# Hybrid attention and convolution layer: x loaded by channels, queries from rows not yet normalised, the operand rescaled later

## The chip, the cores and the metric

The kernel runs on one core of a Trainium2 chip. The metric is the device time of one execution in microseconds (us). Before the change three runs gave 733.79, 735.06 and 737.27 us, median 735.06.

## The reference

One decoder layer over 1024 tokens of 1024 channels. The rows are normalised, projected once, and the projection's columns go to two groups of heads: sparse attention (queries, three pairs of keys and values, gates) and a short gated convolution.

```python
h = rms_norm(x, norm_w)                       # x * rsqrt(mean(x*x) + eps) * norm_w
proj = einsum('bsd,de->bse', h, w_in)
q, kv_all, gate_logits, nsa_z, cv_h, cv_b, cv_c, cv_z = split(proj)
q = apply_rope(rms_norm(q per head, q_norm_w), pos)
k_c, v_c, k_s, v_s, k_w, v_w = split(kv_all, 6)
k_c = rope(rms_norm(compress_blocks(k_c, ...)));  v_c = compress_blocks(v_c, ...)
k_s, k_w = rope(rms_norm(k_s)), rope(rms_norm(k_w))
# compressed, selected and sliding-window attention, gated and summed
o_nsa = (g0 * o_cmp + g1 * o_slc + g2 * o_win) * silu(nsa_z)
o_conv = cv_b * (conv3(cv_c * cv_h) + conv_b) * silu(cv_z)
return x + concat(o_nsa, o_conv) @ w_out
```

Since the queries are normalised once more per head, the row's factor enters them only through the small eps; it is kept all the same, in the statistics.

## The kernel before

Every product is made of three matmuls over a high and a low part of each operand (`three`, L1221 to L1226): high by high, low by high, high by low. `hh` and `hl` are the two parts of the normalised x, stored by channels (128 channels by 1024 tokens, eight blocks), and `wh`, `wl` those of the weights, in two slots.

The first stage, up to about 195 us, works through a list of entries, `ENTRIES`, in this order: q (heads 0 to 3), kc (keys and values that are to be compressed), q (heads 4 to 7), w1 (first hidden layer), kv (selection keys and values), w1 (second hidden layer), kv (window keys and values, and gates), z. An entry of kind q or kv has eight items, one for each 128 tokens, of 256 or 280 columns; kc and z have four items of 512 columns. Items take turns in the four PSUM banks `pj`; an item may start when ScalarE (`act_rel`) and VectorE (`dve_rel`) have read the item that had its bank.

The opening: for each of eight token tiles a transfer brings 128 rows of x, ScalarE squares them with a running sum, VectorE makes the reciprocal standard deviation (`inv_std`) and scales the rows (L973), TensorE transposes them in eight matmuls (`x_transposes`, L1235), ScalarE casts the transposed tile to `hh` (L720) and VectorE subtracts to get `hl` (L980). One tile behind, TensorE computes the first q item.

The weights come in pieces through a ring of four raw buffers (`weights`): SyncE starts a transfer, ScalarE casts it to the high part (L633), GpSimd subtracts to get the low part (L535), and only then the buffer is loaded again. Each engine's order is written out by hand. VectorE normalises queries and keys in place when an entry is through (`normalise`: L916 to L920, L1000, L1001, L925 to L930), TensorE transposes the keys (`key_transposes`, L1294), ScalarE and VectorE split them (`key_hi`, `key_lo`). The kc items are copied into blocks (L666, L667, L955, L956), get a position added (L1042), are cast and subtracted (`block_hi` L695, `block_lo` L547) and feed the hidden layers.

Behind the first stage a main loop of steps does attention, side tiles (convolution and gates; `channels`, written to `pf`) and the output projection. The first side tile's matmuls and the first queries' transposes (L1306) open it.

Of the kernel before, what the change touches and what calls it, by code (L numbers as in the profile page):

```python
# [15 lines left out]
P = 128  # L16
# [17 lines left out]
ENTRIES = [("q", 0, 256, 0), ("kc", 512, 256, 0), ("q", 256, 256, 1), ("w1", 0, 256, 0),  # L34
           ("kv", 768, 256, 0), ("w1", 1, 256, 1), ("kv", 1024, 280, 1), ("z", 1304, 256, 0)]
# [6 lines left out]
PIECES = [5 if w == 280 else 4 for _, _, w, _ in ENTRIES]  # L42
# [7 lines left out]


# [199 lines left out]
def hybrid_layer(nc: bass.Bass, x, wpack, wside, wout, normw, qnorm, knorm, par, const, maskc, out):  # L251
    with ExitStack() as ctx:
# [11 lines left out]
        prm = sb("prm", [P, NPAR])  # L264
        kst = sb("kst", [P, 2, GROUPS, SEQ], F32R)
# [13 lines left out]
        with ExitStack() as c:  # L279
# [3 lines left out]
            with ExitStack() as d:  # L283
                wh, wl = [None, None], [None, None]
                for s in range(2):
                    wh[s] = sb(f"wh{s}", [P, NK * (280 - 24 * s)], F32R, d)
                    wl[s] = sb(f"wl{s}", [P, NK * (280 - 24 * s)], F32R, d)
                sq = sb("sq", [P, 512], F32, d)
# [3 lines left out]
                stat = sb("stat", [P, 5, 41], F32, d)  # L292
# [38 lines left out]
        x_in = [sem(f"x_in{s}") for s in range(2)]  # L331
# [3 lines left out]
        x_sq, x_std, x_norm = sem("x_sq"), sem("x_std"), sem("x_norm")  # L335
        xt_done, hh_ready, hl_ready = sem("xt_done"), sem("hh_ready"), sem("hl_ready")
# [41 lines left out]
        xtile = lambda t: stage[:, (t % 2) * SEQ:(t % 2 + 1) * SEQ]  # L378
        krow = stage.rearrange("p (t g u d) -> p t g u d", t=NT, g=GROUPS, u=2)
        blocks = [mixn[:, 2 * f:2 * f + 2, :] for f in range(2)]  # L380
        hid = mixn[:, 0, 0:4 * P].rearrange("p (a c) -> p a c", a=4)
        ckr = mixn[:, 1, 0:2 * HD].rearrange("p (u d) -> p u d", u=2)
        cksq = mixn[:, 1, 2 * HD:3 * HD]
        cktmp = mixn[:, 1, 256:288].rearrange("p (a r) -> p a r", a=4)
# [11 lines left out]
        def entry_through(eng, e):  # L396

            if ENTRIES[e][0] == "w1":
                eng.wait_ge(hid_done, ENTRIES[e][3] + 1)
            else:  # L400
                eng.wait_ge(item_done, first_item[e + 1])
# [36 lines left out]
        def half_free(eng, h):  # L438

            if h < 3:  # L440
                entry_through(eng, NE - 2)
# [9 lines left out]
        def _(sp):  # L451
            sp.dma_start(xtile(0), x[0:P, :]).then_inc(x_in[0], 16)
            sp.dma_start(cst[:, :], const).then_inc(const_in, 16)
            sp.dma_start(mixc[:, 0, :], normw.to_broadcast([P, DM])).then_inc(normw_in, 16)
            sp.dma_start(xtile(1), x[P:2 * P, :]).then_inc(x_in[1], 16)
# [10 lines left out]
            for p in range(4):  # L466
                weights(p)
            sp.dma_start(prm[:, :], par).then_inc(param_in, 16)
            sp.dma_start(hnorm[:, 0, :], qnorm.to_broadcast([P, HD])).then_inc(param_in, 16)
            for b in range(3):  # L470
                sp.dma_start(hnorm[:, 1 + b, :], knorm[b:b + 1, :].to_broadcast([P, HD])).then_inc(param_in, 16)
            sp.dma_start(maskb[:, :].bitcast(U16), maskc).then_inc(masks_in, 16)
            for t in range(2, NT):
                sp.wait_ge(xt_done, 2 * (t - 2) + 2)
                sp.dma_start(xtile(t), x[t * P:(t + 1) * P, :]).then_inc(x_in[t % 2], 16)
                if t == 4:
                    for p in range(4, 8):
                        weights(p)
            for p in range(8, FIRST_PIECE[NE]):
                weights(p)  # L480

            entry_through(sp, NE - 2)
# [38 lines left out]
        def _(pool):  # L521
# [9 lines left out]
            def weights(p):  # L531
                e, j = PIECE_OF[p]
                w = piece_width(e)
                pool.wait_ge(wh_ready, p + 1)
                nc.gpsimd.tensor_tensor(wl[e % 2][:, j * w:(j + 1) * w], raw[p % 4][:, 0:w],  # L535
                                        wh[e % 2][:, j * w:(j + 1) * w].bitcast(F32), ALU.subtract)\
                    .then_inc(wl_ready, 1)

# [33 lines left out]
            for e in range(NE):  # L572
                for p in range(FIRST_PIECE[e], FIRST_PIECE[e + 1]):
                    weights(p)
                if e == 2:
                    block_lo(0)
                if e == 4:
                    block_lo(1)
            for h in range(3):
                half_lo(h)  # L580
            entry_through(pool, NE - 1)
# [39 lines left out]
        def _(act):  # L621
            A = nc.scalar.activation

            def weights(p):
# [4 lines left out]
                w = piece_width(e)  # L629
                act.wait_ge(raw_in[p % 4], 16 * (p // 4 + 1))  # L630
                if e >= 2:
                    entry_through(act, e - 2)
                nc.scalar.copy(wh[e % 2][:, j * w:(j + 1) * w], raw[p % 4][:, 0:w]).then_inc(wh_ready, 1)  # L633

            def pieces(e):

                return range(FIRST_PIECE[e], FIRST_PIECE[e + 1]) if e < NE else ()

            def item(e, m):
# [3 lines left out]
                bank = pj[n % 4]  # L643
                act.wait_ge(item_done, n + 1)
                if kind in ("q", "kv"):
                    tk = n - sum(items_of(a) for a in range(e) if ENTRIES[a][0] not in ("q", "kv"))
                    w = 256 if kind == "q" else 128
                    if tk >= 2:
                        act.wait_ge(sq_read, tk - 1)
                    A(sq[:, (tk % 2) * 256:(tk % 2) * 256 + w], bank[:, 0:w], ACT.Square).then_inc(sq_ready, 1)  # L650
# [890 lines left out]
```

## Time and profile before

| what | value |
|---|---|
| median of three runs | 735.06 us |
| the profiled execution | 732.45 us, span 730.7 us |
| TensorE busy | 681.3 us, 93% of the span |
| VectorE busy | 468.9 us, 64% |
| ScalarE busy | 372.7 us, 51% |
| GpSimd busy | 197.7 us, 27% |
| mean granted TensorE clock | 0.995 of 2.4 GHz |
| end of the first stage (first side tile) | 194.75 us |

How to read it: the page tells each engine's busy time over the whole span. Matmuls are pipelined, so the distance between their starts, not the duration shown, is what each one costs. In the rows below PE is TensorE, DVE VectorE, ACT ScalarE, POOL GpSimd; L is a line of the kernel; names are those of the program (`qp` holds raw weights, queries and keys, `xt` and `pj` are PSUM banks). A time in brackets is the engine's idle time ahead of the instruction, with what ended it.

### The profile page before, as it was taken

To read this page: it belongs to the slowest core of one execution; us is meant where nothing else is said; L and a number is where in the kernel's file an instruction comes from. 1 tells how busy PE (TensorE), PEld (TensorE's weight loads), DVE (VectorE), ACT (ScalarE), POOL (GpSimd) and SP (SyncE) were. 2 spreads that over 40 slices of the span, in tenths; PEclk is the share of its full clock that TensorE was granted. 3 is DMA by queue.
4 is the path that set the end of the run, shared out by engine and by line. 5 is a ranking of instruction groups with operands and counts; after the bars stand their busy time and mean duration, and the time that the engine had idled before them with its cause. 6 is when DMAs were issued, how large, how long until landed. Compare 5 with 4: busy or idle time off the path is not lost.

```text
span 730.7 us, 10838 instructions
## 1 busy us (share of the span) xinstructions
PE 681.3 (93%) x3791; PEld 575.9 (79%) x3791; DVE 468.9 (64%) x1147; ACT 372.7 (51%) x905; POOL 197.7 (27%) x220
## 2 busy tenths in 40 slices
PE   2899999889999999999998999889899999999997
PEld 1888899888788788878876788778677888888775
DVE  4777454645234655577667787687878777777752
ACT  5652535442334434436564565645677555555541
POOL 2112454520223223133121232211376021212120
PEclk9999999999999999999999999999999999999999
DMA  6521131400111111111100111000042011110101
GB/s 223 174 87 30 30 101 27 110 1 30 44 30 46 42 30 44 31 44 29 30 16 14 30 31 30 14 30 31 33 140 88 30 44 44 44 44 30 59 29 58
DMA packets 19206, 36.85 MB, mean 50 GB/s; under 512 B 2640, under 2 KB 3536, under 8 KB 19152
## 3 DMA queue, kind: packets, MB, share of 16 engines
q1 hardware_dynamic: 19152, 36.15, 15.8%
q8 instruction: 31, 0.51, 0.3%
q14 instruction: 23, 0.19, 0.1%
HBM read 31.95 MB, written 4.19 MB: 49 GB/s over the span
## 4 chain that ended last, share of the span: by engine, by line
PE 75%; DVE 13%; issue 5%; ACT 5%; DMA 2%; POOL 1%; SPq 0%; ACTq 0%; DVEq 0%; POOLq 0%
PE pf L1224 9%; PE pf L1225 9%; PE pf L1226 9%; PE tp L1455 7%; PE po L1435 5%; PE pj L1224 5%; PE pj L1225 5%; PE pj L1226 5%; PE sc L1315 4%; PE po L1436 4%; PE sc L1314 4%; PE sc L1224 3%; PE sc L1226 3%; PE sc L1225 3%; DVE sc L1144 1%
## 5 line engine op out<-in xcount | busy, mean ns | idle before, releaser
L837 ACT CAST pth<-tp 128x512 fp32r<-128x512 f32 (+1 forms) x148 | 86.7, 586 | 130.9 <-PE tp L1455 130.4
L1144 DVE CUSTOM_DVE_ANT_0 sc<-sc,maskb 128x64 f32<-128x64 f32 (+8 forms) x192 | 102.8, 563 | 57.0 <-PE sc L1315 56.6
L1163 DVE TENSOR_TENSOR ptl<-tp,pth 128x512 fp32r<-128x512 f32 (+1 forms) x148 | 102.0, 689 | 45.7 <-ACT pth L837 44.8
L594 POOL TENSOR_SCALAR qp<-qp,precip,gate 128x64 f32<-128x64 f32 x64 | 38.2, 598 | 207.4 <-DVE precip L1134 207.2
L1455 PE MATMUL tp<-cst,qp 128*128 128x128 f32 (+1 forms) x592 | 88.8, 272 | 3.6 <-issue 2.7
L552 POOL TENSOR_TENSOR fl<-fraw,fh 128x512 fp32r<-128x512 f32 x36 | 47.6, 1323 | 127.9 <-ACT fh L702 127.9
L1224 PE MATMUL pf<-hh,fh 128*128 128x512 f32 x200 | 81.2, 406 | 0.8 <-DVE ub L1103 0.8
L1224 PE MATMUL pj<-wh,hh 128*128 128x256 f32 (+1 forms) x256 | 75.5, 295 | 6.7 <-POOL wl L535 5.4
L1455 PEld LDWEIGHTS tp<-cst,qp 128*128 128x128 f32 (+1 forms) x592 | 68.9, 137 | 13.3 <-issue 3.4
L1225 PE MATMUL pf<-hl,fh 128*128 128x512 f32 x200 | 78.8, 394 | 0.0
L1226 PE MATMUL pf<-hh,fl 128*128 128x512 f32 x200 | 78.6, 393 | 0.0
L1225 PE MATMUL pj<-wl,hh 128*128 128x256 f32 (+1 forms) x256 | 73.9, 289 | 0.0
L1226 PE MATMUL pj<-wh,hl 128*128 128x256 f32 (+1 forms) x256 | 73.7, 288 | 0.0
L1435 PE MATMUL po<-pth,val 128*128 128x512 f32 x132 | 62.9, 477 | 7.6 <-DVE ptl L1163 4.5
L535 POOL TENSOR_TENSOR wl<-qp,wh 128x512 fp32r<-128x512 f32 (+1 forms) x33 | 45.7, 1410 | 89.1 <-ACT wh L633 89.1
L1140 DVE TENSOR_SCALAR qp<-qp,precip,gate 128x640 f32<-128x640 f32 (+7 forms) x96 | 57.8, 602 | 3.6
L1224 PEld LDWEIGHTS pj<-wh,hh 128*128 128x128 f32 x256 | 49.9, 195 | 9.0 <-issue 7.6
L1314 PE MATMUL sc<-kst,qh 128*128 128x512 f32 (+3 forms) x152 | 51.8, 341 | 2.8 <-DVE ql L1016 2.2
L1315 PE MATMUL sc<-kst,ql 128*128 128x512 f32 (+3 forms) x152 | 52.1, 345 | 0.0
L1436 PE MATMUL po<-ptl,val 128*128 128x512 f32 x132 | 52.1, 395 | 0.0
L1224 PE MATMUL pf<-woh,msh 128*128 128x512 f32 x120 | 49.1, 409 | 2.8 <-POOL wol L606 2.6
L1225 PEld LDWEIGHTS pj<-wl,hh 128*128 128x128 f32 x256 | 49.9, 195 | 0.0
(185 smaller groups left out, 1556.3 us busy)
## 6 DMA issues: line engine op xcount, KB each, us to landing
fraw<-in_wside SPq DMA_DIRECT2D x36, 256.0 KB, 2.7
qp<-in_wpack SPq DMA_DIRECT2D x28, 256.0 KB, 3.1
qp<-in_x SPq DMA_DIRECT2D x8, 512.0 KB, 3.3
wor<-in_wout SPq DMA_DIRECT2D x16, 256.0 KB, 2.8
xo<-in_x SPq DMA_DIRECT2D x16, 256.0 KB, 2.8
out<-xo SPq DMA_DIRECT2D x16, 256.0 KB, 2.0
qp<-in_wpack SPq DMA_DIRECT2D x5, 224.0 KB, 2.6
maskb<-in_maskc SPq DMA_DIRECT2D x1, 544.0 KB, 5.8
```

The costliest lines, as they stand in the source:

```text
L837: nc.scalar.copy(pth[ptn % 2][0:r, :], tp[tpn % 2][0:r, :]).then_inc(pth_ready, 1)
L1140: V.tensor_scalar(p, p, factor, main, ALU.mult, ALU.mult).then_inc(p_dve, 1)
L1144: return V.tensor_tensor_reduce(row, row, mask, -1.0, -NEG, ALU.add, ALU.min, most)
L1163: V.tensor_tensor(ptl[ptn % 2][0:r, :], tp[tpn % 2][0:r, :], pth[ptn % 2][0:r, :].bitcast(F32), ALU.subtract).then_inc(tp_read, 1)
L1224: MM(dst, lh, rh, start=start, stop=False)
L1225: MM(dst, lh, rl, start=False, stop=False)
L1226: return MM(dst, ll, rh, start=False, stop=stop)
L1314: MM(dst, qh[:, h, :], keys, start=True, stop=False)
L1315: return MM(dst, ql[:, h, :], keys, start=False, stop=True)
L1435: MM(po[:, :], v, pth[pt % 2][0:r, :], start=first, stop=False)
L1436: MM(po[:, :], v, ptl[pt % 2][0:r, :], start=False, stop=last).then_inc(pv_done, 1)
L1455: ins = nc.tensor.transpose(tp[tpn % 2][0:r, h * P:(h + 1) * P], src, ident)
```

## The change

A transposed copy of x (`xcm`, channels by tokens) becomes a further input, so x is loaded by channels and the transposes of x go. The opening then runs over eight channel blocks. For each block ScalarE writes the high part of x times norm_w (a per-channel factor, so a scale of the copy), without the row's factor, VectorE the low part, ScalarE squares the block and VectorE adds the squares up. The queries, now one entry of 512 columns, are computed from that operand over all eight token tiles at once, one in each of the eight PSUM banks: five channel blocks wide, then the last three tile by tile.

The row's factor comes later: TensorE transposes the summed squares, VectorE reduces them, makes the factor, and multiplies the queries' statistics and the selection keys and values by it. TensorE transposes a broadcast of the factor into rows along the tokens; VectorE multiplies x by them, ScalarE and VectorE or GpSimd write `hh` and `hl` again, one half of the tokens when four selection kv items are done and the other when eight are.

The order of entries becomes q, kv (selection), kc, kv (window), w1, z, w1, and the orders on all engines are written anew: the key transposes lie between kv items, the hidden layers between kv and z items, the query normalisations between kv items and between z items. Some scratch gets buffers of its own.

```diff
-ENTRIES = [("q", 0, 256, 0), ("kc", 512, 256, 0), ("q", 256, 256, 1), ("w1", 0, 256, 0),
-           ("kv", 768, 256, 0), ("w1", 1, 256, 1), ("kv", 1024, 280, 1), ("z", 1304, 256, 0)]
+ENTRIES = [("q", 0, 512, 0), ("kv", 768, 256, 0), ("kc", 512, 256, 0), ("kv", 1024, 280, 1),
+           ("w1", 0, 256, 0), ("z", 1304, 256, 0), ("w1", 1, 256, 1)]
 # SyncE
+            weights(0)
+            for hf in range(2):
+                sp.dma_start(xk(0)[:, hf * 512:(hf + 1) * 512], xcm[0:P, hf * 512:(hf + 1) * 512]).then_inc(x_in[NK * hf], 16)
+            for k in range(1, NK):
+                sp.dma_start(xk(k), xcm[k * P:(k + 1) * P, :]).then_inc(x_in[k], 16)
+                weights(k)
 # GpSimd
+            for e in (E_Q, E_KV0, E_KC):
+                entry_weights(e)
+            for hf in range(2):
+                scaled_lo(hf)
+            entry_weights(E_KV1)
+            block_lo(0)
+            entry_weights(E_W0)
+            entry_weights(E_Z)
+            block_lo(1)
+            entry_weights(E_W1)
 # ScalarE
+                    A(hh[:, k, cols], xk(k)[:, cols], ACT.Copy, scale=nw[:, k:k + 1]).then_inc(hh_ready, 1)
+            def scaled_hi(hf, ks):
+                cols = slice(hf * 512, (hf + 1) * 512)
+                act.wait_ge(item_done, first_item[E_KV0] + 4 * (hf + 1))
+                for k in ks:
+                    act.wait_ge(xs_ready, 8 * hf + k + 1)
+                    nc.scalar.copy(hh[:, k, cols], xk(k)[:, cols]).then_inc(hs_ready, 1)
+            keys_hi(0, 0, 0)
+            for p in pieces(E_W0):
+                weights(p)
+            keys_hi(2, 0, 0)
 # VectorE
+            for m in range(NT):
+                item(E_KV0, m)
+                if m in (2, 3):
+                    rescale(0, range(4 * m - 8, 4 * m - 4))
+                if m == 4:
+                    rescale(1, range(2))
+                    scaled_lo(0)
+                if m in (5, 6):
+                    rescale(1, range(3 * m - 13, 3 * m - 10))
+            scaled_lo(1)
+            normalise_k(0)
+            for m in range(4):
+                item(E_KC, m)
+                if m == 1:
+                    positions(0)
+            keys_lo(0, 0, 0)
+            positions(1)
+            keys_lo(2, 0, 0)
 # TensorE
-            for t in range(NT + 1):
-                if t < NT:
-                    x_transposes(t)
-                if t >= 1:
-                    item(0, t - 1)
+            for k in range(Q_WIDE):
+                query_wide(k)
+            for t in range(NT):
+                query_tile(t)
+                if t == NT - 2:
+                    sums_transposes()
+            for m in range(NT):
+                item(E_KV0, m)
+                if m == 1:
+                    rows_transposes()
+            for m in range(4):
+                item(E_KC, m)
+            key_transposes(0, 2, 0, 1)
+            item(E_KV1, 0)
+            key_transposes(2, 4, 0, 1)
+            for m in range(1, 4):
+                item(E_KV1, m)
+            hidden(E_W0, 0)
+            for m in range(4, NT):
+                item(E_KV1, m)
+                if m == 5:
+                    compressed(0)
+            item(E_Z, 0)
...
+            item(E_Z, 1)
+            hidden(E_W1, 1)
+            key_transposes(0, 2, 5, 3)
+            item(E_Z, 2)
+            key_transposes(2, 4, 5, 3)
+            compressed(1)
+            item(E_Z, 3)
```

## Rows read from the trace of the kernel before

**Rows 1.** Busy times by stretch: length, engines' busy us (instructions), clock, DMA share, GB/s.

```profile
21.00:53.00 32.00, 28.41 (x224) 26.30 (x224) 23.75 (x49) 19.30 (x45) 5.15 (x4) 1.00 0.39 133
53.00:100.00 47.00, 45.19 (x291) 41.24 (x291) 24.15 (x39) 18.51 (x36) 16.59 (x10) 1.00 0.16 45
100.00:146.00 46.00, 41.88 (x345) 40.95 (x344) 28.50 (x52) 22.06 (x53) 25.30 (x15) 1.00 0.27 72
146.00:150.00 4.00, 1.06 (x10) 0.83 (x9) 2.84 (x15) 1.80 (x4) 0.00 (x0) 1.00 0.01 2
150.00:155.00 5.00, 5.00 (x29) 4.81 (x28) 2.83 (x9) 3.21 (x10) 1.82 (x2) 0.66 0.00 0
```

**Rows 2.** Groups by line and form, 0 to 200 us: busy, mean ns | idle, releasers.

```profile
L1235 PE MATMUL xt<-cst,qp 128*128 128x128 f32 x64 | 10.4, 315 | 17.2 <-DVE qp L973 17.2
...
L973 DVE SCALAR_TENSOR_TENSOR qp<-qp,stat,mixc 128x1024 f32<-128x1024 f32 x8 | 11.2, 1406 | 0.3
```

**Rows 3.** Timeline of PE, opening: start, us, instruction [idle before, releaser].

```profile
16.35 1.97 PE L1235 MATMUL xt<-cst,qp 128*128 128x128 f32 x8 [4.70 <-DVE qp L973]
...
22.03 1.03 PE L1235 MATMUL xt<-cst,qp 128*128 128x128 f32 x8
```

**Rows 4.** Timeline of PE, first matmuls of items.

```profile
69.64 0.39 PE L1224 MATMUL pj<-hh,wh 128*128 128x512 f32 x1
...
75.08 0.28 PE L1224 MATMUL pj<-wh,hh 128*128 128x256 f32 x1
...
79.99 0.28 PE L1224 MATMUL pj<-wh,hh 128*128 128x256 f32 x1
...
82.87 0.28 PE L1224 MATMUL pj<-wh,hh 128*128 128x256 f32 x1
```

**Rows 5.** Timeline of PE, key transposes and end of the first stage.

```profile
149.74 1.73 PE L1294 MATMUL xt<-cst,qp 128*128 128x128 f32 x8 [2.94 <-DVE kst L964]
...
194.75 0.48 PE L1224 MATMUL pf<-hh,fh 128*128 128x512 f32 x1
...
198.43 0.63 PE L1306 MATMUL tp<-cst,qd 128*128 128x128 f32 x4 [0.70 <-POOL qd L562]
```

**Rows 6.** Timeline of DVE, first key normalisation, POOL busy.

```profile
133.70 0.17 DVE L916 TENSOR_SCALAR stat<-stat 128x16 f32<-128x16 f32 x1 [1.33 <-ACT stat L735]
...
136.51 2.11 DVE L1000 TENSOR_TENSOR qp<-qp,stat 128x1024 f32<-128x1024 f32 x1
...
143.00 0.76 DVE L1070 COPY qp<-qp 128x512 f32<-128x512 f32 x2
```

**Rows 7.** Timeline of DVE, second key normalisation, POOL idle.

```profile
172.35 0.17 DVE L916 TENSOR_SCALAR stat<-stat 128x16 f32<-128x16 f32 x1
...
173.35 1.23 DVE L1000 TENSOR_TENSOR qp<-qp,stat 128x1024 f32<-128x1024 f32 x1
...
177.34 0.76 DVE L1070 COPY qp<-qp 128x512 f32<-128x512 f32 x2
```

**Rows 8.** Timeline of POOL, block and weight subtractions.

```profile
118.81 5.78 POOL L547 TENSOR_TENSOR xcl<-mixn,xch 128x1024 fp32r<-128x1024 f32 x2 [9.65 <-ACT xch L695]
...
124.50 5.10 POOL L535 TENSOR_TENSOR wl<-qp,wh 128x512 fp32r<-128x512 f32 x4
...
134.20 7.48 POOL L535 TENSOR_TENSOR wl<-qp,wh 128x448 fp32r<-128x448 f32 x5 [4.60 <-ACT wh L633]
```

**Rows 9.** Timeline of ACT, casts of weights and blocks.

```profile
101.45 2.16 ACT L633 CAST wh<-qp 128x512 fp32r<-128x512 f32 x4
...
114.88 3.85 ACT L695 CAST xch<-mixn 128x1024 fp32r<-128x1024 f32 x2
...
138.07 0.57 ACT L633 CAST wh<-qp 128x448 fp32r<-128x448 f32 x1 [2.54 <-DMA qp<-in_wpack]
```

**Rows 10.** DMA over 0 to 30 us in 40 slices, GB/s.

```profile
GB/s 0 0 126 344 370 314 229 202 355 366 391 396 408 345 357 362 171 313 360 11 0 0 0 0 0 38 229 410 22 0 0 0 153 393 377 328 377 399 186 328
```

**Rows 11.** Groups by line and form, 0 to 200 us, blocks of kc.

```profile
L1042 DVE TENSOR_TENSOR mixn<-mixn,prm 128x1024 f32<-128x1024 f32 x4 | 5.7, 1483 | 0.0
...
L955 DVE COPY mixn<-pj 64x512 f32<-64x512 f32 x4 | 2.8, 693 | 6.6 <-PE pj L1226 6.6
```

More of the change, by code:

```diff
@@ new lines, in _, with root @@
+            A(stat[:, 1, S_ONE:S_ONE + 1], stat[:, 0, S_ONE:S_ONE + 1], ACT.Sqrt)
+            def root(lo, count, width, done):
+                A(stat[:, 1, lo:lo + count], stat[:, 0, lo:lo + count], ACT.Sqrt, scale=1.0 / width,
+                  bias=cst[:, C_EPS:C_EPS + 1]).then_inc(done, 1)
+            act.wait_ge(normw_in, 16)
+            for k in range(NK):
+                weights(k)
+                channel_hi(k)
+                if k >= 1:
+                    channel_sq(k - 1)
+            channel_sq(NK - 1)
@@ L738, in _ @@
+            root(S_KV, 16, HD, head_std)
+            act.wait_ge(q_sums, 1)
+            root(0, 64, HD, head_std)
+            for p in pieces(E_KV1):
+                weights(p)
             tpn = ptn = 0
@@ new lines, in _ @@
+            for p in pieces(E_Z):
+                weights(p)
+            block_hi(1)
+            for m in range(4, NT):
+                item(E_KV1, m)
+                if m == 5:
+                    act.wait_ge(cmp_done, 1)
+                    A(cksq[:, :], xt[3][:, 0:HD], ACT.Square).then_inc(ck_raw, 1)
+                    nc.scalar.copy(ckr[:, 0, :], xt[3][:, 0:HD]).then_inc(ck_raw, 1)
+                    act.wait_ge(ck_sum, 1)
+                    root(S_CK, 1, HD, ck_std)
+            act.wait_ge(sq_read, 3 * NT)
@@ new lines, in _ @@
+            root(S_KV + 16, 16, HD, head_std)
+            act.wait_ge(gate_raw, NT)
+            A(gate[:, :, :], gate[:, :, :], ACT.Tanh, scale=0.5).then_inc(gate_tanh, 1)
+            for p in pieces(E_W1):
+                weights(p)
+            item(E_Z, 0)
+            act.wait_ge(kt_done, 5)
+            nc.scalar.copy(kend[:, :, P:P + CB], xt[0][:, 0:P].rearrange("p (g c) -> p g c", g=GROUPS)).then_inc(kt_hi, 1)
+            item(E_Z, 1)
+            hidden(1)
+            keys_hi(0, 5, 1)
@@ new lines, in _ @@
+            channel_add(NK - 1)
+            for m in range(NT):
+                item(E_Q, m)
+            dve.wait_ge(sums_turned, 2)
+            for hf in range(2):
+                ins = V.tensor_reduce(stat[:, 0, S_X + 4 * hf:S_X + 4 * hf + 4],
+                                      xt[hf][:, :].rearrange("p (t c) -> p t c", t=4), AX.X, ALU.add)
+            ins.then_inc(x_sum, 1)
+            inv_std(S_X, NT, DM, x_std, 1)
+            r = stat[:, 2, S_X:S_X + NT]
+            rsq = stat[:, 4, S_X:S_X + NT]
@@ L1087, in side @@
+            item(E_Z, 3)
             def side(f):
```

608 lines of the change are left out of this document (337 added, 271 removed).

## The prediction

> **What bounds the kernel now.** I read the busy times by stretch first [rows 1]. The kernel is a long main loop behind a first stage that ends when TensorE (PE) starts the first side tile at 194.75 us [rows 5]. The change touches nothing behind that point, so its worth is the distance by which that moment moves. In the first stage PE is the busiest engine, but not without holes: it is idle for 3.6 us of 21 to 53 us (32.00 less 28.41), 1.8 of 53 to 100, 4.1 of 100 to 146 and 2.9 of 146 to 150, about 12.4 us in all [rows 1]. Next I read the opening by line: the transposes of x are 64 matmuls, 10.4 us busy, and PE stood idle 17.2 us ahead of them, always waiting for VectorE's (DVE's) normalised row tile, L973 [rows 2]. Steady work begins only with the second tile, at 16.35 us [rows 3]. Last come the pace of PE [rows 4], the stall ahead of the key transposes with the clock behind it [rows 1, 5], and the same DVE chain with GpSimd (POOL) busy and with POOL idle [rows 6 to 8].
>
> **What goes from PE's work.** A 256-column item lasts 2.88 us (79.99 to 82.87) for 24 matmuls, 0.12 each; a 512-column item 5.44 (69.64 to 75.08), 0.227 each [rows 4]. Queries cost 16 x 2.88 = 46.1 us now and 8 tiles x 24 x 0.227 = 43.5 after: 2.6 less. From 16.35 us on the transposes of x cost 8.5 (the row's 10.4 less the first eight, 1.9); what replaces them, eight transposes of the squared sums and eight of the broadcast rstd, is two groups at 1.03 [rows 3], 2.1. So 2.6 + 6.4 = **9.0 us of PE work less**. Everything else on PE (keys and values, hidden layers, z, key transposes) has the same matmuls in another order.
>
> **The earlier start.** The first matmul needs one 256 KB piece of weights, half a channel block of x (256 KB) and the 4 KB of norm weights, no constants, statistics or transposes. In the opening, cut into 40 slices of 0.75 us, the first bytes move in the third (1.5 to 2.25 us), and most busy slices then show 310 to 410 GB/s [rows 10]; 0.5 MB at that rate take 1.5 us, so with the landing about 4.5 us; then come a cast (2.16 for four, 0.54 each [rows 9]) and a scaled copy of the same size. I take 6 us for PE's first matmul, with 5 and 8 as bounds. Against 16.35 that is **10.3 us earlier**. The half-rate opening of the clock is paid once in either kernel.
>
> **Does the supply keep up?** Each of the eight channel steps costs PE 24 x 0.227 = 5.44 us. It needs 768 KB (2.2 us at 350 GB/s); on ScalarE (ACT) one cast of 512 columns and one scaled copy and one square of 1024, five times 0.54, some 2.7 us; on DVE one split and one add of 1024 columns, by L973 1.28 to 1.41 each [rows 2], 2.8 us, some 4 with POOL in its way; on POOL one subtraction, 1.3 to 1.5 (5.10 for four alone, 7.48 for five beside DVE [rows 8]). All lie below 5.44, so PE sets the pace: q runs from 6 to 52.3 us (43.5, two more for the slow clock, and the sums' transposes inside). Rotating over eight banks has no row; a change of bank between matmuls of the main stage costs nothing visible, and the dearest change of group (transposes to matmuls) some 0.1 us, so the bounds are 0 and 192 x 0.1 = 19 us. I take 0, since the change of bank alone is the nearer case.
>
> **Where the chain runs after q.** Sums, square root and rstd: two reductions, a root, five small operations (172.35 to 173.35, 1.0 us [rows 7]) and two broadcast copies (0.4 each, as the pair of L1070 [rows 7]); with 0.7 for each reduction and each PSUM read ahead of them I estimate 5.5 us behind the last q tile, so 58 us. They are covered by the first two kv items (2 x 2.88 from 52.3), and PE loses at most 0.5. Kv ends near 76.5. Then kc needs the operand rescaled in place: 16 DVE products (half of L973's 1.28 to 1.41, so 0.7 [rows 2]) and 16 ACT casts of 512 columns (0.54), 8 subtractions on DVE (0.7) and 8 on POOL (5.10 for four, 1.3 each [rows 8]). The second half may be overwritten only when the last kv item is done. Its casts run 77 to 83, and kc's first item (5.44, to 81.9) covers them if DVE is on time. Here DVE and POOL meet. With POOL busy on 448-column subtractions (7.48 us [rows 8]) DVE's product L1000 took 2.11 us against 1.23 with POOL idle, and the whole key normalisation 133.70 to 143.76, 10.1, against 172.35 to 178.10, 5.8 [rows 6, 7]. During 134.2 to 141.7 the two engines nearly took turns. The Trainium skill, page "SBUF — State Buffer", section "Who interferes with whom", calls the port pair that DVE operations with two SBUF inputs share with POOL "an exclusive lock"; by that rule it speaks against this change, which splits x out of SBUF twice where L980 read one operand from PSUM, and in full it gives the 752 us of rival (c). The trace agrees as to sign (2.11 against 1.23), and by its own loss the sum is the forecast. With turns taken, DVE's low half of the rescale is done at 83.5 to 87.5 instead of 80 to 83, and PE loses **3.5** in kc's second item.
>
> **The second wait** lies at the selection keys. DVE: normalise keys at the slow price, 88 to 98; four copies of kc at 0.69, 2.8; positions, 2.9 (L955, and two of the four of L1042 [rows 11]), to 103.6. ACT: the 3.85 cast of the blocks [rows 9], kc's last four copies, and only then the first key cast, near 110.5; the fifth kv piece, for which ACT waited 2.54 on a transfer [rows 9], returns here because the ring of four raw buffers is refilled only after POOL's subtraction, but it is covered by DVE's chain. By 106 PE has done kc (101.9), the first two groups of key transposes and one kv item, and the other two groups stand in its queue ahead of the remaining seven kv items. They need both key subtractions: **5.2 us** lost. **The third**: the second hidden layer needs its weights' low part, which POOL gives only behind the second block subtraction (5.78 [rows 8]) and ACT's late casts, near 154.5, with PE ready at 150.8: **3.7**. The query normalisations (some 9 us each, an estimate from the 5.8 of rows 7 at twice the columns) are moved behind kv items on DVE; each holds back bank releases, but four banks and the hidden layer between cover that. Small waits (ckr transposes, last key transposes): about 1.1. Sum of stalls 13.5 against 12.4 now.
>
> **Clock.** After the 2.9 us hole at 146 to 150 the granted clock averaged 0.66 over 150 to 155 [rows 1], the lower level (1.2 GHz) for two thirds of it: 1.7 us lost. Two holes of that size after the change (5.2 and 3.7) cost 3.4 against 1.7 now.
>
> **The sum.** Start 10.3 earlier, work 9.0 less, stalls 1.1 more, clock 1.7 more: 16.5. Then the 0.7 us wait for the copied queries at 198.43 [rows 5] goes, since POOL's and DVE's part is done while the last z item runs, and half of kc's loss may be overlapped: 17 to 20. I take 19. The profiled execution lasted 732.45 us (span 730.7), which gives 713.5; the median of the runs, 735.06, lies 0.36% above it and gives 716. I forecast 715.
>
> **Rivals.** (a) DVE and POOL hardly collide and the placed order fits: the stalls shrink from 13.5 to about 2 and the clock never falls. That is 11.5, and 3.4 of clock, less the half of kc's loss already taken: 13 us more, 702. For it: POOL has only some 45 us of work between 60 and 155; against it: rows 6. (b) Queueing doubles the stalls: every step behind 76 us is in fixed order on ACT and DVE, and a cast held for one PE result holds the next three. 13.5 more, with one more clock drop: 730. For it: ACT's blocks cast and the hidden activation stand ahead of key casts and kv releases. (c) Slower: the take-turns price is paid on the path wherever POOL works between 60 and 155. The place is DVE's rescale, both key normalisations, positions and the compressed-key chain; the price is POOL's time there, 8 x 1.3 + 5 x 1.5 + 12 x 1.3 + two block subtractions of 5.8 each [rows 8], 45 us, of which the forecast has 8 on the path (3.5 at kc, 4.3 in the key normalisation). If all of the other 37 lands, 715 + 37 = 752; it turns slower once more than some 24 of them do. Against it: in the window of rows 6 DVE lost only 4.3 for 7.48 of POOL; I put this case at 745. (d) The wide stage doesn't deliver: each change of bank costs up to 0.1 us, 19 us, about 734, no change.
>
> **How the numbers follow.** Forecast 715 (706 to 724): 0.62. (a) 702: 0.15. (b) 730: 0.13. (c) 745: 0.05. (d) 734: 0.05. The range 701 to 731 keeps the forecast, a part of (a) and of (b), and leaves out about 0.2. A measurement of this kernel tells about 0.5% (3.7 us) from no change. Faster: 0.62 + 0.15 + most of (b), 0.87; within: (d) and the end of (b), 0.07; slower: (c) and a rest for what I don't see, 0.06.
>
> **What would show it.** Right: PE's first matmul near 6 us and q done near 52; no PE hole over 0.5 between 8 and 76; a hole of some 5 us at the second pair of key transposes near 106; first side tile near 175; the main loop as long as before. Wrong: holes in the wide stage (supply or banks), DVE's 512-column products well over 1.3 us each, or a first side tile behind 190.

## The result, and the profile after

The changed kernel takes 717.36 us (median of four runs, 713.15 to 717.95), the kernel before 734.42 (733.79 to 737.27). The ratio is 0.9753, 95% interval 0.9717 to 0.9788: faster by 2.5%. The forecast was 715, range 701 to 731. The profiled execution of the changed kernel lasted 717.58 us, span 715.8; that of the kernel before 732.45, span 730.7. So 14.9 us are to be found in the traces.

First the page: span, PE's and DVE's busy time, and the granted clock in 40 slices of 17.9 us. In PEclk a full slice shows 9; the fifth (72 to 89 us) and the ninth (143 to 161) stand at 8, the tenth (161 to 179) at 7.

```profile
span 715.8 us, 10320 instructions
PE 676.8 (95%) x3551; PEld 564.3 (79%) x3551; DVE 491.1 (69%) x1122; ACT 376.9 (53%) x882; POOL 218.1 (30%) x228
PEclk9999899987999999999999999999999999999999
```

Next the timeline of PE: start, us, instruction, and in brackets the idle time before it with its releaser. The first row answers to [rows 3], the pair at 28 us to [rows 4], the others to [rows 5].

```profile
6.45 2.05 PE L1414 MATMUL pj<-wh,hh 128*128 128x512 f32 x4 [6.45 <-ACT hh L687]
...
28.07 1.07 PE L1421 MATMUL pj<-wl,hh 128*128 128x512 f32 x4
28.98 1.07 PE L1421 MATMUL xt<-wl,hh 128*128 128x512 f32 x4
...
81.62 0.47 PE L1380 MATMUL pj<-hh,wh 128*128 128x512 f32 x1 [0.22 <-POOL hl L576]
...
87.20 0.77 PE L1380 MATMUL pj<-hh,wh 128*128 128x512 f32 x1 [4.65 <-DVE hl L1082]
...
113.59 1.17 PE L1501 MATMUL xt<-cst,qp 128*128 128x128 f32 x8 [3.11 <-DVE kst L1052]
...
156.20 0.30 PE L1380 MATMUL xt<-xch,wh 128*128 128x128 f32 x1 [3.06 <-issue]
...
181.11 0.39 PE L1380 MATMUL pf<-hh,fh 128*128 128x512 f32 x1
```

PE begins at 6.45 us. The pair at 28 us shows the wide queries: four matmuls of 512 columns on four banks start 0.91 us after the four before, 0.227 each, the pace of [rows 4]; the change of bank costs nothing. Kv starts at 52.55 and kc at 76.44. Three holes follow, in kc (0.22 and 4.65), at the second key transposes (3.11) and ahead of the second hidden layer (3.06), 11.0 us in all. The first side tile starts at 181.11 instead of 194.75, 13.6 earlier. From there to the end of the span it is 534.7 us against 535.9.

The windows around the holes give busy time and number of instructions by engine, then granted clock, DMA share and GB/s:

```profile
80.00:100.00 20.00, 15.05 (x54) 10.48 (x53) 19.44 (x32) 7.76 (x16) 15.12 (x10) 0.83 0.24 65
140.00:160.00 20.00, 16.94 (x86) 14.68 (x84) 18.00 (x42) 8.27 (x22) 11.15 (x6) 0.91 0.06 18
160.00:180.00 20.00, 20.00 (x93) 17.94 (x93) 12.07 (x21) 5.09 (x12) 3.88 (x3) 0.74 0.19 54
```

The last row is the one the forecast had nothing for: PE is busy for all of its 20 us, no hole in it, and the clock averages 0.74. It stood at its lower level, 1.2 GHz, from 156.6 to 170.2.

Now the engines behind the first hole, DVE's rescale and its subtractions beside POOL's eight subtractions, from the timelines of DVE and POOL:

```profile
71.40 1.40 DVE L1074 SCALAR_TENSOR_TENSOR xlow<-xlow,nw,mixn 128x512 f32<-128x512 f32 x2
72.72 2.49 DVE L1082 TENSOR_TENSOR hl<-xlow,hh 128x512 fp32r<-128x512 f32 x4
...
80.70 4.68 DVE L1074 SCALAR_TENSOR_TENSOR mixc<-mixc,nw,mixn 128x512 f32<-128x512 f32 x3
...
85.76 6.07 DVE L1082 TENSOR_TENSOR hl<-xlow,hh 128x512 fp32r<-128x512 f32 x4
...
72.35 15.84 POOL L576 TENSOR_TENSOR hl<-mixc,hh 128x512 fp32r<-128x512 f32 x8 [4.01 <-ACT hh L701]
```

DVE's product costs 0.70 early (1.40 for two) and 1.56 at 80.7 us (4.68 for three); its subtraction 0.62 (2.49 for four), then 1.52 (6.07 for four). POOL's row averages 2.0 us where the forecast had 1.3 [rows 8], and the average hides two stretches: the first subtraction took 4.01 us, while DVE ran its own four back to back at 0.62; the other seven took 1.7 each, in step with DVE's products. So POOL was held up first, and both from then on. PE's item waits for the subtractions at 85.76, which start only when the products are through.

### The profile page after: what moved, and what is told of

It reads as the page before. It is cut to its first block, busy times and chain, and to the rows that moved or that the text cites. A ratio compares the mean times of both kernels' runs of the same rounds, so it can differ in the third digit from the quotient of the medians.

```text
span 715.8 us, 10320 instructions
## 1 busy us (share of the span) xinstructions
PE 676.8 (95%) x3551; PEld 564.3 (79%) x3551; DVE 491.1 (69%) x1122; ACT 376.9 (53%) x882; POOL 218.1 (30%) x228
## 4 chain that ended last, share of the span: by engine, by line
PE 78%; DVE 13%; issue 4%; ACT 3%; POOL 1%; DMA 1%; SPq 0%; ACTq 0%; DVEq 0%
PE pf L1380 10%; PE pf L1381 9%; PE pf L1382 9%; PE tp L1673 7%; PE po L1653 5%; PE sc L1522 4%; PE po L1654 4%; PE sc L1521 4%; PE sc L1380 3%; PE sc L1382 3%; PE sc L1381 3%; PE pj L1380 3%; PE pj L1381 3%; PE pj L1382 3%; DVE sc L1300 1%
## 5 line engine op out<-in xcount | busy, mean ns | idle before, releaser
L565 POOL TENSOR_TENSOR wl<-qp,wh 128x512 fp32r<-128x512 f32 (+1 forms) x33 | 50.2, 1543 | 59.0 <-ACT wh L676 59.0
L1522 PE MATMUL sc<-kst,ql 128*128 128x512 f32 (+3 forms) x152 | 52.3, 347 | 0.0
L902 ACT ACTIVATE qp<-sc,nmax 128x128 f32<-128x128 f32 (+7 forms) x64 | 47.5, 743 | 3.2 <-DVE nmax L1300 3.1
L1380 PEld LDWEIGHTS pf<-hh,fh 128*128 128x128 f32 x200 | 37.7, 188 | 12.2 <-issue 2.2
L1381 PE MATMUL pf<-wol,msh 128*128 128x512 f32 x120 | 47.1, 393 | 0.0
L1382 PE MATMUL pf<-woh,msl 128*128 128x512 f32 x120 | 47.1, 392 | 0.0
L1382 PEld LDWEIGHTS pf<-hh,fl 128*128 128x128 f32 x200 | 37.8, 189 | 8.8
```

The lines of the kernel that those rows point to most:

```text
L1380: MM(dst, lh, rh, start=start, stop=False)
L1381: MM(dst, lh, rl, start=False, stop=False)
L1382: return MM(dst, ll, rh, start=False, stop=stop)
L1522: return MM(dst, ql[:, h, :], keys, start=False, stop=True)
```

## The experiments

The theory: the gain is the earlier start and the lighter queries, one for one; the loss is DVE and POOL taking turns, above all in kc; and the clock behind the holes costs more than the forecast had. The rivals: the length of DVE's queue, not POOL, makes the first hole; the end of the first stage is set by another chain, so the early start or the filled holes are worth little; the clock's cost belongs to a hole whatever follows it. Line numbers move by a few where lines were taken out.

### The early start

Does the start count in full? TensorE's first matmul is made to wait for the constants as well.

```diff
+            pe.wait_ge(const_in, 16)
             for k in range(Q_WIDE):
                 query_wide(k)
```

> Nothing left out; TensorE's first matmul waits for the constants as well, which SyncE requests behind all channel blocks of x (they land near 20 us). All loads, casts, splits and squares go on as before. Theory (PE sets the pace of the opening, the earlier start counts one for one): PE starts near 20 instead of 6.45 us, q ends near 65 to 66, and the first side tile and the end come 12 to 15 us later, the execution at 729 to 733. Rival (the opening is bound by ACT's and DVE's channel work, which an early PE only waits for): the delay is swallowed by half or more, 720 to 724.

Measured: 732.87 us, beside 734.29 for the kernel before. The timeline of PE:

```profile
21.46 2.07 PE L1414 MATMUL pj<-wh,hh 128*128 128x512 f32 x4 [21.46 <-DMA cst<-in_const]
...
102.92 0.76 PE L1380 MATMUL pj<-hh,wh 128*128 128x512 f32 x1 [4.65 <-DVE hl L1082]
...
171.91 0.30 PE L1380 MATMUL xt<-xch,wh 128*128 128x128 f32 x1 [1.83 <-issue]
...
195.25 0.39 PE L1380 MATMUL pf<-hh,fh 128*128 128x512 f32 x1
```

PE starts 15.0 us later than in the changed kernel, the first side tile comes 14.1 later and the execution ends 15.3 later. The closer pair is the changed kernel's second execution (changed_again, below), in which the clock fell at the same three holes: 15.3 of start became 15.1 at the first side tile. The start is worth all but one for one. It starts 5.1 us later than the kernel before did, and the first side tile is only 0.5 behind that one's: the rest of the change is worth some 4.6 by itself.

### DVE and POOL at kc

Two kernels ask who makes the first hole. One leaves POOL's eight subtractions out, so kc's products use old low parts there; the other gives the same eight to DVE, which then has more to do, with POOL idle.

```diff
-            for hf in range(2):
-                scaled_lo(hf)            # GpSimd
```

> Left out: GpSimd's eight subtractions that renew the low part of channel blocks 4 to 7 after the rescale (those low parts keep the values of the first pass). Theory (taking turns): the 4.65 us hole in kc's second item is there because DVE's products and subtractions and POOL's subtractions share a way into SBUF (three products took 4.68 us, 1.56 each, against 0.66 where POOL is idle). Without POOL the products take 0.65 to 0.70, DVE is through with the low half near 83 us, the hole at 82.6 us falls under 1 us, the clock stays at its upper level there, and kc ends near 98 to 99 instead of 106.4. The wait ahead of the second key transposes then stands at 3 to 5 us and the first side tile comes at 172 to 176 instead of 181. Rival (queue length): DVE has simply too many operations between 63 and 92 us; then the hole stays at 3 us or more although POOL is quiet.

```diff
-            for hf in range(2):
-                scaled_lo(hf)            # GpSimd
 # VectorE
...
-                    scaled_lo(0)
+                    scaled_lo(0, range(4))
+                if m == 5:
+                    scaled_lo(0, range(4, NK))
-            scaled_lo(1)
+            scaled_lo(1, range(NK))
...
```

> The eight subtractions of POOL are moved to DVE (nothing left out). Theory (taking turns): a POOL subtraction of 512 columns blocks DVE for about 1.3 us, and done by DVE it costs 0.62, so DVE with eight more operations is still earlier: low half done at 88 instead of 91.8 us, hole near 82 down from 4.65 to about 2, first side tile 2 to 5 us earlier, 176 to 179. Rival (queue length): eight more operations on the engine that is late make the hole longer, 5 us more, and the first side tile comes at 184 or later.

Without the eight: 709.93 us, no hole in kc. The timeline of its DVE, at the place of the two slow groups above:

```profile
78.97 2.06 DVE L1072 SCALAR_TENSOR_TENSOR mixc<-mixc,nw,mixn 128x512 f32<-128x512 f32 x3
...
81.41 2.48 DVE L1080 TENSOR_TENSOR hl<-xlow,hh 128x512 fp32r<-128x512 f32 x4
```

The same instructions cost 0.69 and 0.62 each again. With the eight on DVE: 711.83 us, and the timeline of PE shows

```profile
84.90 0.47 PE L1380 MATMUL pj<-hh,wh 128*128 128x512 f32 x1 [1.62 <-DVE hl L1080]
...
112.11 1.30 PE L1498 MATMUL xt<-cst,qp 128*128 128x128 f32 x5 [6.64 <-DVE kst L1050]
```

DVE does eight subtractions more and the hole in kc falls from 4.87 to 1.62 us. So it was not the length of DVE's queue. PE now reaches the second key transposes 5 us earlier, at 105.5 instead of 110.5, and waits there 6.64 us instead of 3.11: what was gained ahead of a chain in fixed order on ScalarE and DVE is partly given back there. The size was measured again over several rounds.

> lo_all_dve once more, now with an interval. Theory of turns taken: 710 to 713 us median, 5 to 6 less than the changed kernel's 717.36, ratio to the kernel before about 0.968. Rival: the longer wait at the second key transposes (6.64 us) gives most of it back in other executions: 714 to 717.

Measured: 710.87 us (708.3 to 712.03), ratio 0.968, interval 0.9662 to 0.9697. This interval lies wholly below that of the changed kernel. GpSimd's share of the rescale costs more than it saves.

### The clock behind the third hole

Fourteen matmuls into a bank that is overwritten later are put into the third hole, ahead of the second hidden layer (48 matmuls of 128 columns).

```diff
             item(E_Z, 1)
+            ...                          # the wait for that bank
+            for _ in range(14):
+                MM(pj[last % 4][:, :], wh[SLOT[E_Z]][:, 0:P], hh[:, 0, 0:512], start=True, stop=True)
             hidden(E_W1, 1)
```

> Nothing left out; 14 matmuls of 512 columns whose result is overwritten later are put between the second z item and the second hidden layer, where PE stood idle from 153.1 to 156.2 us. Theory (clock): the hole itself costs 3.1 us, but the half-rate stretch behind it (granted clock 0.50 from 157 to 170 us) costs more: the 48 matmuls of the hidden layer took 11.5 us against 5.3 at the upper level. With the hole filled the clock stays up and the layer takes 5.3 to 5.6 although it starts no earlier; the first side tile comes 3 to 6 us earlier (the last key chain on DVE gives some back). Rival (layer slow for another reason, as its operands or its 128-column form): the layer still takes over 10 us and the first side tile stays at 181.

Measured: 715.28 us, which lies among the changed kernel's own executions; what shows is the stretch in the trace. With no hole the clock stays at 1.00 there and the hidden layer takes 5.3 us instead of 9.9 (the 11.5 of the expectation has the eight key transposes behind it in). From the start of the first z item to the first side tile it is 32.56 us against 39.15, 6.6 less. The windows that answer to those of the changed kernel above:

```profile
140.00:160.00 20.00, 20.00 (x112) 17.51 (x110) 17.70 (x44) 9.22 (x27) 11.90 (x6) 1.00 0.10 28
160.00:180.00 20.00, 20.00 (x123) 17.67 (x122) 13.90 (x22) 5.70 (x13) 5.17 (x7) 1.00 0.23 66
```

But here the hole at the second key transposes (2.98 us) was followed by the lower clock until 120.3, where 3.11 us had not been in the changed kernel.

The same hole can be filled with useful work, the third z item:

```diff
             item(E_Z, 1)
+            item(E_Z, 2)
             hidden(E_W1, 1)
             key_transposes(0, 2, 5, 3)
-            item(E_Z, 2)
```

> Nothing left out; the third z item goes ahead of the second hidden layer and its key transposes on TensorE. It fills the hole at 153 to 156 us with 5.4 us of real work. Theory (clock and hole): the hidden layer starts at 158.6 and takes 5.3; then the last key transposes wait for DVE's queue, which has the second query normalisation first (to 165.6) and the hidden layer's steps and key subtractions behind (to 169.5), so a new hole of some 4 us opens ahead of them; first side tile at 176 to 178, 3 to 5 us earlier, not 9. Rival (hole only, no new wait): 172.

Measured: 714.47 us, again among the changed kernel's own; from the first z item to the first side tile 33.07. The hidden layer again runs at the full clock. A new hole opens where the item was taken away, 1.85 us at the last pair of key transposes (some 4 were expected), with the lower clock behind it.

What holds the clock down for 13 us, the hole or what follows it? The fourteen matmuls now stand behind the hole, between the hidden layer's waits and its first matmul. Beside it the changed kernel runs once more, to see how much of this differs from execution to execution.

```diff
             def hidden(e, f):
                 ...
                 if f == 1:
                     pe.wait_ge(hid_pre, 1)
+                    ...                  # the wait for that bank
+                    for _ in range(14):
+                        MM(pj[last % 4][:, :], wh[SLOT[E_Z]][:, 0:P], hh[:, 0, 0:512], start=True, stop=True)
```

> Fourteen matmuls of 512 columns into a bank that is overwritten later stand behind the third hole, ahead of the second hidden layer's 48 matmuls of 128 columns (in fill_third_hole they stood ahead of the hole). Theory: the clock stayed at 1.2 GHz for 13 us because narrow matmuls followed the hole, so with wide ones it is back some 4 to 5 us after PE starts again, as behind the hole in kc, and the hidden layer takes 5.3 to 6 us; from the first z item to the first side tile 37 to 40 us, against 39.2 in the changed kernel, although 14 matmuls were added. Rival: the clock needs its 13 us whatever runs; then the fourteen cost about 6 us at the lower clock on top, and the stretch takes about 45 us.

> The changed kernel once more, unchanged. Its executions lay between 713.15 and 717.95 us. Theory: the holes come out alike (4.65, 3.1 and 3.1 us within 0.3), but whether a hole of about 3 us is followed by the lower clock differs from one execution to the next, so the stretches at 1.2 GHz need not be the two of the first profile. Rival: the clock is set by the program alone, so the hole at the second key transposes keeps the full clock again, the one ahead of the second hidden layer loses it for about 13 us, and the first side tile lies at 181 within 0.5.

Measured: 718.14 us with the fourteen, 717.01 without. First the windows of the changed kernel's second execution (its hole is 1.76 us, PE starts again at 156.80):

```profile
155.00:157.50 2.50, 0.74 (x8) 0.73 (x7) 2.46 (x5) 0.00 (x0) 1.70 (x2) 1.00 0.00 0
157.50:160.00 2.50, 2.50 (x17) 2.50 (x16) 2.40 (x6) 0.60 (x1) 0.00 (x0) 0.62 0.04 7
160.00:162.50 2.50, 2.50 (x14) 2.50 (x13) 2.47 (x2) 0.00 (x0) 0.00 (x0) 0.50 0.00 0
162.50:165.00 2.50, 2.50 (x13) 2.50 (x13) 2.47 (x5) 0.00 (x0) 0.00 (x0) 0.50 0.00 0
165.00:167.50 2.50, 2.50 (x15) 2.50 (x14) 2.12 (x6) 0.28 (x1) 0.00 (x0) 0.50 0.17 25
```

then those with the fourteen behind the hole (1.84 us, PE starts again at 157.20), and that stretch in its timeline:

```profile
155.00:157.50 2.50, 0.66 (x3) 0.30 (x2) 2.46 (x4) 0.00 (x0) 2.10 (x2) 1.00 0.00 0
157.50:160.00 2.50, 2.50 (x9) 1.97 (x8) 2.40 (x7) 0.54 (x1) 0.00 (x0) 0.67 0.03 7
160.00:162.50 2.50, 2.50 (x11) 2.04 (x10) 2.47 (x2) 0.06 (x1) 0.00 (x0) 0.65 0.00 0
162.50:165.00 2.50, 2.50 (x25) 2.50 (x24) 2.47 (x3) 0.00 (x0) 0.00 (x0) 1.00 0.00 0
165.00:167.50 2.50, 2.50 (x24) 2.50 (x24) 2.26 (x6) 0.00 (x0) 0.00 (x0) 1.00 0.00 0
...
157.20 5.03 PE L1483 MATMUL pj<-hh,wh 128*128 128x512 f32 x14 [1.84 <-issue]
```

Same hole, same fall, PE busy throughout in both. With 128-column matmuls the clock stood at 0.50 from 158.1 to 168.3, through those 48 and eight key transposes, and rose when 512-column matmuls had run for 0.9 us; with 512-column ones first it was back at 161.7, while they ran, and stayed at 1.00 through the 48 narrow ones. This is one execution; beside it stand four in which the narrow ones came first (the changed kernel twice, no_pool_lo and late_start), all with 10.2 to 13.7 us at the lower level. From the first z item to the first side tile it is 36.3 us with the fourteen and 36.3 without: 14 matmuls were added for nothing. The rival, a fixed price of the hole, would have made it some 6 us longer.

The second execution was forecast less well. The holes of 4.65 and 2.82 us came as expected, and the second was followed by the lower clock this time, as the theory allowed. The third was 1.76 and not 3.06: PE came 1.9 us later (0.6 at kc, the rest by the clock behind the second hole), and the chain that ends the third hole only 0.6 later, 156.80 against 156.20. So what an early hole costs is partly taken back at a later one, and executions with other drops end within 0.6 us of each other.

### Both at once, and another order

The two best edits together (the low parts on DVE, the third z item ahead of the hidden layer):

> Nothing left out; the low halves all on DVE and the third z item ahead of the second hidden layer, together. Theory (DVE's queue is next late): in the run with the low halves on DVE the hole ahead of the second hidden layer was 0.5 us only, and the last key transposes waited 0.8 for DVE; the z item fills a hole that is gone, so the two gains do not add: first side tile 173 to 175, as with the low halves alone (174.3). Rival (they add): 170 to 171.

Measured: 711.19 us, first side tile at 174.68. They don't add: holes of 1.62, 6.70 and 1.90 us remain, and the gains ahead of them are lost in them. The next kernel keeps the low halves on DVE and moves what waits in the last two. ScalarE casts the first keys ahead of the compressed blocks; on PE one more kv item goes ahead of the second key transposes, the first hidden layer behind the sixth kv item, the third z item ahead of the second hidden layer and the fourth ahead of the last key transposes:

```diff
             for m in range(4):           # ScalarE
                 item(E_KC, m)
-                if m == 1:
-                    block_hi(0)
             keys_hi(0, 0, 0)
+            block_hi(0)
 # TensorE
             item(E_KV1, 0)
+            item(E_KV1, 1)
             key_transposes(2, 4, 0, 1)
             ...
             item(E_Z, 1)
+            item(E_Z, 2)
             hidden(E_W1, 1)
             key_transposes(0, 2, 5, 3)
-            item(E_Z, 2)
+            item(E_Z, 3)
             key_transposes(2, 4, 5, 3)
             compressed(1)
-            item(E_Z, 3)
```

> Nothing left out; the low halves on DVE, and the order changed in three places: ACT casts the first two key groups ahead of kc's blocks; on TensorE the second pair of key transposes comes behind the second kv item instead of the first, and the first hidden layer behind the sixth; the third z item comes ahead of the second hidden layer and the fourth ahead of the last key transposes. Theory (the 6.6 us hole at 105 to 112 us is made by the order, ACT's block cast standing ahead of the key casts, and DVE's queue is not yet the bound): that hole falls under 1.5 us, its clock drop (some 3 us) goes, DVE's chain starts some 3 us earlier, first side tile at 166 to 171, execution 702 to 707. Rival (DVE's chain of normalisations is the bound behind 110 us): the hole only moves behind the first hidden layer, first side tile at 173 or later, 709 to 712.

Measured: 710.3 us (709.25 to 711.02), ratio 0.9666, interval 0.9622 to 0.971. It beats both the kernel before and the changed one, but not measurably lo_all_dve, and it misses the 702 to 707 that was expected. The hole at the keys is gone: DVE's first key subtractions start at 105.64 us instead of lo_all_dve's 111.28. Which of the moves did it no run separates, but those subtractions wait for ScalarE's casts. The first side tile lies at 170.85, just inside the 166 to 171 expected, and other holes have come. Part of the miss lies behind that point: from there to the end of the span it is 536.6 us against the changed kernel's 534.7, with 6.8 us at the lower clock there against 3.4. The same order with POOL keeping its eight subtractions:

> Nothing left out; the same new order, but with the low halves of channel blocks 4 to 7 on POOL as in the changed kernel. Theory (taking turns is its own loss, apart from the order): the hole in kc's second item is there again (4 to 5 us, and its clock drop), first side tile 4 to 8 us behind the run with the low halves on DVE, 172 to 177. Rival (order is all): within 2 us of it.

Measured: 711.34 us, first side tile at 173.74, 2.9 behind; the holes in kc are back (0.23 and 4.64). That is between the two expectations, and not all of it is POOL's: PE starts 0.66 us later in this execution and its clock rises later (at 11.2 us instead of 9.05), so kc's first matmul, which the rescale has not yet held up, comes 1.4 later already. Some 1.5 are left for POOL's share. PE's holes up to the first side tile add up to 9.1 us here and 9.0 there, since the holes in kc come in place of the one at the kv items (3.08). One execution, 1.0 us above the other kernel's median, doesn't tell the two apart.

Where the new order's gain went is told by the rows around its longest hole, PE's, DVE's and POOL's timelines:

```profile
116.96 0.37 PE L1379 MATMUL pj<-wh,hh 128*128 128x280 f32 x1 [3.08 <-DVE val L1033]
...
106.97 7.78 DVE L1176 TENSOR_TENSOR mixn<-mixn,prm 128x1024 f32<-128x1024 f32 x2
...
140.57 2.72 DVE L996 TENSOR_TENSOR stat<-stat 128x1 f32<-128x1 f32 x1
...
106.90 6.77 POOL L587 TENSOR_TENSOR xcl<-mixn,xch 128x1024 fp32r<-128x1024 f32 x2 [13.86 <-ACT xch L761]
...
137.54 5.74 POOL L587 TENSOR_TENSOR xcl<-mixn,xch 128x1024 fp32r<-128x1024 f32 x2 [0.29 <-ACT xch L761]
```

Kv releases wait behind two additions that take 7.78 us beside POOL's block subtraction, and one operation on one column per partition takes 2.72. The last run leaves POOL's block subtractions out.

```diff
-            block_lo(0)                  # GpSimd
-            block_lo(1)
 # TensorE, hidden layers
-                    ins = three(..., xch[:, l, :], xcl[:, l, :],
+                    ins = three(..., xch[:, l, :], xch[:, l, :],
```

> The order of reordered with GpSimd's two block subtractions (about 6 us each) left out; the products that used the low part of the blocks take the high part in its place, so TensorE's work is the same. Theory: these subtractions hold up VectorE's positions, normalisations and compressed chain and so make the holes of 3.08 and 0.83 us; without them the first is under 1.5, the second under 0.3, the first side tile at 166 to 168.5 and the execution at 703.5 to 706.5 us. Rival: ScalarE's order (key and block casts in one queue) sets these holes; then they shrink by less than 0.7 together, and the first side tile stays at 170 to 171.

Measured: 703.99 us, clock 1.00 throughout the first stage after the opening. Its DVE, at the same two places, and its first side tile on PE:

```profile
108.58 3.46 DVE L1163 TENSOR_TENSOR mixn<-mixn,prm 128x1024 f32<-128x1024 f32 x2
...
137.28 0.16 DVE L983 TENSOR_TENSOR stat<-stat 128x1 f32<-128x1 f32 x1
...
166.55 0.53 PE L1365 MATMUL pf<-hh,fh 128*128 128x512 f32 x1 [1.81 <-DVE vcmp L1219]
```

The holes of 3.08 and 0.83 us are gone, those of 1.63, 1.65 and 1.81 stay, and the first side tile is 4.3 us earlier, at 166.55. So POOL's block subtractions, not ScalarE's order, held these two holes open. (The edit also drops the waits for the low part; both holes waited for DVE, and DVE's operations at these places are the shorter ones.) This isn't a version to use, since the blocks' low part is missing; it prices 12.5 us of POOL work (6.77 and 5.74) that lies off the path by every count of busy time at 4 to 6 us of the path.

## Why the prediction was right, and the step that failed

**The start** (forecast 6 us, 10.3 earlier): 6.45, 9.9 earlier, and late_start shows that it counts in full. **PE's work** (9.0 less, q done at 52.3, kv at 76.5): 52.55 and 76.44. Supply, banks and the covered rstd chain were costed at nothing and cost nothing: no idle row between 6.45 and 76.44. Rival (d) falls with the pair at 28 us. Of the signs that the forecast gave, two went against it: the first side tile came at 181 and not near 175, and DVE's 512-column products took 1.56 us, over the 1.3 that it had named as a sign of being wrong.

**The three holes** were named where they came. Kc was put at 3.5 and measured 4.87; the keys at 5.2 and measured 3.11, since PE reached them at 110.5 and not at 106; the hidden layer at 3.7 (150.8 to 154.5) and measured 3.06 (153.14 to 156.20). The small waits, 1.1, didn't come. Together 11.0, where 13.5 was forecast. That POOL is the cause at kc is shown by no_pool_lo and lo_all_dve. The half of kc's loss that was to be overlapped, 1.75, was not.

At the third hole the timelines of POOL, DVE and ACT agree with the cause named in the forecast and add one link. The chain is read from them; no run takes it apart.

```profile
139.31 5.80 POOL L587 TENSOR_TENSOR xcl<-mixn,xch 128x1024 fp32r<-128x1024 f32 x2 [0.33 <-ACT xch L763]
...
142.34 2.79 DVE L999 TENSOR_TENSOR stat<-stat 128x1 f32<-128x1 f32 x1
...
147.48 0.31 ACT L777 ACTIVATE stat<-stat,cst 128x16 f32<-128x16 f32 x1 [4.45 <-DVE stat L1026]
...
150.05 6.05 POOL L565 TENSOR_TENSOR wl<-qp,wh 128x512 fp32r<-128x512 f32 x4 [4.95 <-ACT wh L676]
```

DVE's operation on one column per partition starts at 142.34 and ends at 145.13, as POOL's second subtraction does (145.11); 0.16 us is its price with POOL idle. ScalarE, ahead of whose weight casts a root and a table load stand, waits 4.45 us for DVE's statistics behind it, and so POOL's last weights come late. The Trainium skill, page "SBUF — State Buffer", section "Summary: rules for kernel authors", says that a VectorE instruction with two SBUF inputs and a GpSimd one that reads SBUF exclude each other: the second to issue is blocked until the first has finished. This pair agrees, 2.79 us against 0.16.

**The clock** is the term that was mis-sized. The forecast took one loss, 1.7 us behind a hole of 2.9 [rows 1], and gave it to each of two holes, 3.4. Measured in the profiled execution: behind the first hole the clock is at 1.2 GHz from PE's restart at 87.20 to 91.73, half of which, 2.3, is lost; behind the third from 156.6 to 170.2, 6.8 lost; 9.1 in all. Two things failed in this step. It gave a drop to the holes at the keys and the hidden layer and, without a reason, none to kc's, which it had put at 3.5 us, longer than the 2.9 of its row. The 4.65 us hole in kc was followed by the lower clock in all seven profiled executions that have it; the one at the keys in five of the six that have it, the first being the exception. And it took the loss for a property of the hole. In the row that it was read from, eight transposes and then 280-column matmuls came behind the hole; behind the third hole come 48 matmuls and eight transposes of 128 columns, and the clock stayed down until 512-column ones ran. Fill_after_hole shows, in one execution, that with the hole unchanged the loss is another one.

**The sum.** To the first side tile: 9.9 of start, 9.0 of work, 1.4 of holes (12.4 less 11.0), less 7.4 of clock (9.1 less 1.7), 12.9; the traces show 13.6. The forecast for that point was 19 less the 0.7 of the queries, 18.3. It missed by 4.7 there: 5.7 of clock, 1.75 of overlap and 0.4 of start too good, 2.5 of holes too bad, and 0.7 that the terms leave open. The holes came out shorter than forecast and hid a part of the clock's error; that is luck. Behind that point 1.2 us were gained, where the 0.7 us for the queries was forecast.

That the median, 717.36, lies so near to 715 owes something to the executions: between the two profiled ones 14.9 us were gained, between the medians 17.1.

**The rivals.** (a), 702 without collisions: no run removes them all. Without POOL's eight subtractions alone the changed order takes 709.93; reordered_no_block_lo, with its block subtractions gone too, comes to 703.99, but in another order, so how right the price was stays open. (b), doubled stalls, didn't come. (c), the turn-taking as the main loss, has the right mechanism and a far smaller size: where POOL works for 15.8 us at the rescale, PE stood 4.9, and it then waited 3.1 at the keys where it waits 6.6 with the low halves on DVE.

Open: why a hole of 3.11 us kept the full clock in one execution, when 2.82, 2.98, 3.08 and 1.67 lost it in others. The runs show that it differs between executions of one kernel and not what decides it. The spread of a kernel's times goes with it: the changed kernel's 713.15 us has a mean granted clock of 0.988, its 717.14 to 717.95 one of 0.983.

## What to carry to other kernels

Price work on GpSimd by what it does to VectorE: subtractions that look free on an idle engine doubled the time of VectorE's products beside them, and giving them to VectorE, or leaving them out, made the kernel faster. Where a matmul chain must wait, fill the hole with useful work, or put useful 512-column matmuls directly behind it and narrow ones after: the same 48 narrow matmuls took 9.9 us one way and 5.3 the other in these traces. When the gain of a fix is partly given back, look for the next fixed-order chain behind it; here early gains of 5 us came out as 3.5 more of waiting at the keys.

## What the runs showed of the hardware beyond the forecast

TensorE, busy without a gap, stayed at 1.2 GHz for 10.2 and 13.7 us in the changed kernel's two executions, while 56 matmuls of 128 columns ran, and rose 0.9 and 2.5 us after 512-column ones began; with fourteen 512-column ones first it was back 4.5 us after its restart. A hole of 1.67 us (no_pool_lo, at 148.06) was followed by the lower clock, and so was one of 1.76; one of 3.11 was not. Two holes of 1.8 us at the same place, ahead of the first side tile, differed as well: the clock stayed up in reordered and fell in reordered_pool. One VectorE operation on a single column per partition took 2.79 us beside a GpSimd subtraction of 1024 columns, 0.16 without.
